# Stacking the meta rows of four heads on one operand's partitions, and regrouping the small steps of the input projection

## The reference

```python
h = rmsnorm(h_res, pre_mix_g)                     # (272, 2048)
q_da, k_da, v_da, q_g, k_g, v_g, g_g, lr_g = split_cols(h @ w_in)
o_da = diff_attention(...)    # 8 heads: p = softmax(q0 k0) - lam * softmax(q1 k1), causal; o = p @ v
                              # then rmsnorm over the head's 128 features
o_gla = gla(...)              # 4 heads, chunks of 64: A = tril(q_in k_in^T); o = A v + q_in S_prev
                              # then rmsnorm over the head's 256 features, times silu(g)
h_res = h_res + rmsnorm(concat[o_da, o_gla] @ w_out, post_mix_g)
y = conv_ffn(rmsnorm(h_res, pre_ffn_g), w_up, conv_w, conv_b, w_down)   # causal conv, width 3
h_res = h_res + rmsnorm(y, post_ffn_g)
return h_res[:, 16:]
```

## Time and profile before

| | |
|---|---|
| median of 3 runs | 1217.77 us (1217.37 to 1217.83) |
| the profiled execution | 1217.71 us, span 1216.0 us, mean granted clock 0.998 |
| input projection (96 slots) | to about 353 us of the span |
| PE, DVE, ACT, POOL busy | 1203.3, 662.5, 605.4, 478.2 us |

### The profile page before, as it was taken

One profiled execution on the slowest core, in us unless ns is written; L12 is line 12 of the kernel. 1 busy time (PEld: TensorE's weight loads), 2 busy tenths in 40 slices (PEclk: granted clock), 3 DMA queues, 4 the chain that ended last, 5 costly groups with the idle time before them and its releaser, 6 DMA issues.

```text
span 1216.0 us, 23728 instructions
## 1 busy us (share of the span) xinstructions
PE 1203.3 (99%) x8948; PEld 1145.3 (94%) x8948; DVE 662.5 (54%) x961; ACT 605.4 (50%) x908; POOL 478.2 (39%) x221
## 2 busy tenths in 40 slices
PE   9999999999999999999999999999999999999997
PEld 9999999999999999999999999999999988888885
DVE  7765555554565347766666666656656643232234
ACT  7544445455674447554445444444444544444444
POOL 1233333323424433444444444444444444444443
PEclk9999999999999999999999999999999999999999
DMA  9655554544536655566565565665655665665651
GB/s 330 201 156 156 141 161 143 148 130 132 153 124 197 193 164 159 173 189 182 178 185 177 177 188 174 188 186 168 193 181 169 191 203 184 199 191 189 197 166 70
DMA packets 175695, 212.31 MB, mean 175 GB/s; under 512 B 6688, under 2 KB 162720, under 8 KB 175520
## 3 DMA queue, kind: packets, MB, share of 16 engines
q1 hardware_dynamic: 175216, 210.32, 56.4%
q10 hardware_dynamic: 432, 1.34, 0.3%
HBM read 209.53 MB, written 2.10 MB: 174 GB/s over the span
## 4 chain that ended last, share of the span: by engine, by line
PE 95%; DVE 2%; ACT 2%; DMA 1%; issue 0%; SPq 0%; DVEq 0%; ACTq 0%
PE psum L416 69%; PE psum L1776 19%; PE psum L1416 1%; PE psum L1646 1%; DMA raw<-in_w_in 1%; PE psum L1476 1%; ACT w_hi L396 1%; PE psum L1804 0%; PE psum L1502 0%; PE psum L1736 0%; PE psum L1585 0%; DVE w_lo L400 0%; PE psum L1603 0%; PE psum L1503 0%; PE psum L1598 0%
## 5 line engine op out<-in xcount | busy, mean ns | idle before, releaser
L400 POOL TENSOR_TENSOR w_lo<-raw,w_hi 128x1024 fp32r<-128x1024 f32 x188 | 463.6, 2466 | 709.3 <-ACT w_hi L396 709.3
L416 PE MATMUL psum<-a_hi,w_hi 128*128 128x258 f32 (+1 forms) x2360 | 675.3, 286 | 0.9 <-ACT temp L594 0.8
L416 PE MATMUL psum<-a_lo,w_hi 128*128 128x258 f32 (+1 forms) x2360 | 673.8, 286 | 0.0
L416 PE MATMUL psum<-a_hi,w_lo 128*128 128x258 f32 (+1 forms) x2360 | 670.1, 284 | 0.0
L396 ACT ACTIVATE w_hi<-raw 128x1024 fp32r<-128x1024 f32 x391 | 411.5, 1059 | 471.6 <-PE psum L416 341.9
L400 DVE TENSOR_TENSOR w_lo<-raw,w_hi 128x1024 fp32r<-128x1024 f32 x204 | 268.7, 1318 | 412.9 <-ACT w_hi L396 411.7
L416 PEld LDWEIGHTS psum<-a_hi,w_hi 128*128 128x128 f32 x2360 | 448.3, 190 | 7.1 <-issue 4.3
L416 PEld LDWEIGHTS psum<-a_lo,w_hi 128*128 128x128 f32 x2360 | 448.5, 190 | 0.0
L416 PEld LDWEIGHTS psum<-a_hi,w_lo 128*128 128x128 f32 x2360 | 446.1, 189 | 0.1
L1306 DVE SCALAR_TENSOR_TENSOR proj<-proj,par 128x256 f32<-128x256 f32 x88 | 111.4, 1266 | 36.1 <-ACT proj L816 36.1
L1776 PE MATMUL psum<-w_hi,a_lo 128*128 128x512 f32 x336 | 130.7, 389 | 0.0
(11 more groups left out here) (234 smaller groups left out, 610.8 us busy)
## 6 DMA issues: line engine op xcount, KB each, us to landing
raw<-in_w_up SPq DMA_DIRECT2D x176, 512.0 KB, 3.6
raw<-in_w_in SPq DMA_DIRECT2D x95, 512.0 KB, 4.5
raw<-in_w_down SPq DMA_DIRECT2D x88, 512.0 KB, 4.1
raw<-in_w_out SPq DMA_DIRECT2D x32, 512.0 KB, 3.7
xT<-in_features SPq DMA_DIRECT2D x3, 544.0 KB, 7.6
temp<-in_post_ffn_g ACTq DMA_DIRECT2D x1, 1024.0 KB, 4.8
out<-proj SPq DMA_DIRECT2D x2, 512.0 KB, 2.7
out<-proj SPq DMA_DIRECT2D x4, 256.0 KB, 2.9
```

Of the source, the lines that this page charges most:

```text
L400: eng.tensor_tensor(w_lo[:, j % SPLIT, :], raw[:, j, :], w_hi[:, j % SPLIT, :], ALU.subtract)\
L416: mm = pe.matmul(psum[:, bank + m, 0:t1 - t0], w[:, j % SPLIT, cols], a[:, k, t0:t1], start=(k == 0 and step == 0), stop=(k == KT - 1 and ...
```

## The change

The 16 meta rows of four heads are put on partitions 0, 32, 64 and 96 (and the 15 after each) of one operand (`rows_of`). For the attention heads `v_meta_rows` then holds two groups of four heads, and `pT_meta_rows` gets one buffer for each of the four positions, zero elsewhere. `c_T` transposes the probabilities of four heads at once, and DVE multiplies them by a block mask (`row_block`) into `c_p_blocks`, so that `c_attend` is two matmuls of 128 rows by 8 columns; `c_attend_rest` is gone. For the GLA heads ACT copies the meta rows of v into `m_v` in every `v_T` step, DVE writes the masked products into `m_a`, and one step `m_o` in slot 89 (two matmuls of 128 rows by 8 columns) takes the place of line 1608 in four steps.

The steps move: `c_scores` 61 to 57, `c_T` 64 to 60, `c_attend` to 63, `c_sums` 67 to 65; DVE's and ACT's part of the normalization is split over slots 66 and 67; `da_o_T` from 69-76 to 68, 73, 73, 76, 81, 81, 84, 89; `gla_o` of the first three heads from +7 to +8, its normalization to +9 and `gla_o_T` from +10 to +11; `m_sums` 92 to 91. The weight stream, its order and its buffers are as they were.

```diff
-    for name, at in (("c_scores", C_BASE), ("c_T", C_BASE + 3), ("c_attend", C_BASE + 4), ("c_attend_rest", C_BASE + 5),
-                     ("c_sums", C_BASE + 6)):
+    for name, at in (("c_scores", C_SLOT), ("c_T", C_T_SLOT), ("c_attend", C_ATTEND_SLOT), ("c_sums", C_SUMS_SLOT)):
         if slot == at:
             steps.append((name, 0))
-    if C_BASE + 8 <= slot < C_BASE + 8 + n_da:
-        steps.append(("da_o_T", slot - C_BASE - 8))
+    steps += [("da_o_T", h) for h in range(n_da) if DA_O_SLOTS[h] == slot]
     for hd in range(n_gla):
-        for name, lag in (("v_T", 0), ("k_T", 3), ("kv", 5), ("gla_o", 7), ("gla_o_T", 10)):
+        for name, lag in (("v_T", 0), ("k_T", 3), ("kv", 5), ("gla_o", o_lag(hd)), ("gla_o_T", o_lag(hd) + 3)):
             if slot == gla_base(hd) + lag:
                 steps.append((name, hd))
+    if slot == M_O_SLOT:
+        steps.append(("m_o", 0))
     if slot == M_SLOT:
         steps.append(("m_sums", 0))
     return steps
...
-            "attend": 1, "c_scores": 2, "c_T": 1, "c_attend": 1, "c_attend_rest": 0, "c_sums": 1, "m_sums": 1, "da_o_T": 1, "v_T": 2, "k_T": 2, "kv": 2, "gla_o": 2,
+            "attend": 1, "c_scores": 2, "c_T": 1, "c_attend": 1, "c_sums": 1, "m_o": 1, "m_sums": 1, "da_o_T": 1, "v_T": 2, "k_T": 2, "kv": 2, "gla_o": 1,
             "gla_o_T": 2}
-C_BASE = 61
+C_SLOT, C_T_SLOT, C_ATTEND_SLOT, C_SUMS_SLOT = 57, 60, 63, 65
+DA_NORM_SLOT = 66
+DA_O_SLOTS = (68, 73, 73, 76, 81, 81, 84, 89)
 X_RMS_SLOT, LR_SLOT = 8, 9
 FIRST_LO = 12
 N_WARM = 12


 SCAN_SLOTS = (14, 16, 20, 22)
-M_SLOT = 92
+M_O_SLOT, M_SLOT = 89, 91


...
     return 60 + 8 * hd
+
+
+def o_lag(hd):
+
+    return 8 if hd < 3 else 7
...
-        m_o = sb("m_o", [P, n_gla, 2, NM])
-        m_sq = sb("m_sq", [P, n_gla, 2, NM])
+        m_o = sb("m_o", [P, 2, n_gla, NM])
+        m_sq = sb("m_sq", [P, 2, n_gla, NM])
+        m_a = sb("m_a", [P, n_gla, NM])
+        c_p_blocks = sb("c_p_blocks", [P, 2, 4, NM])
+        row_block = sb("row_block", [P, 4])
...
         pT_main = pv_buf[:, 2 * P:5 * P]
-        pT_meta_rows = pv_buf[:, 5 * P:7 * P]
-        pT_meta = pT_meta_rows[0:n_meta, :]
+        m_v = pv_buf[:, 5 * P:7 * P].rearrange("p (v e) -> p v e", v=2)
         o_nat = carve(2 * n_da * P).rearrange("p (t h e) -> p t h e", t=2, h=n_da)
-        v_meta_rows = tile(40, 4)[:, 0:n_da * P].rearrange("p (h e) -> p h e", h=n_da)
-        v_meta = v_meta_rows[0:n_meta]
+        stacked = tile(40, 5)[:, 0:10 * P]
+        v_meta_rows = stacked[:, 0:2 * P].rearrange("p (g e) -> p g e", g=2)
+        pT_meta_rows = stacked[:, 2 * P:10 * P].rearrange("p (j k) -> p j k", j=4)
+
+        def rows_of(n):
+
+            return slice(32 * (n % 4), 32 * (n % 4) + n_meta)
+
         c_e = tile(T_V + 7)[0:NM, 0:2 * n_da * n_meta].rearrange("p (c k) -> p c k", k=n_meta)
-        c_p = tile(T_K + 7)[0:NM, 0:n_da * n_meta].rearrange("p (h k) -> p h k", h=n_da)
-        c_pT = tile(T_K + 7)[0:n_meta, n_da * n_meta:(n_meta + NM) * n_da]
+        c_p_rows = tile(T_K + 7)[0:NM, 0:n_da * 32]
+        c_p = c_p_rows.rearrange("p (h k) -> p h k", h=n_da)[:, :, 0:n_meta]
...
+            link(masked(row_block[:], 1.0, [[-32, 4]], 0, 1, ALU.is_ge, 0.0))
+            pool.affine_select(out=row_block[:], in_=row_block[:], compare_op=ALU.is_ge, fill=0.0, base=n_meta - 1,
+                               pattern=[[32, 4]], channel_multiplier=-1).then_inc(consts_made, 1)
+            pool.memset(m_a[:], 0.0).then_inc(consts_made, 1)
...
-                    pool.memset(v_meta_rows, 0.0).then_inc(meta_zeroed, 1)
-                    pool.memset(pT_meta_rows, 0.0).then_inc(meta_zeroed, 1)
+                    pool.memset(stacked, 0.0).then_inc(meta_zeroed, 1)
+                    pool.memset(m_v, 0.0).then_inc(meta_zeroed, 1)
                 for hd in range(n_gla):
...
+                        copy(v_meta_rows[rows_of(h), h // 4, :], psum[0:n_meta, bank_of(step), 0:P]).then_inc(free(step), 1)
...
-                        copy(pT_meta, psum[0:n_meta, bank_of(step, 1), 0:2 * P]).then_inc(free(step, 1), 1)
-                if slot == C_BASE:
+                        copy(pT_meta_rows[rows_of(h), h % 4, :], psum[0:n_meta, bank_of(step, 1), 0:2 * P]).then_inc(free(step, 1), 1)
+                if slot == C_SLOT:
                     act_e.wait_ge(c_shifted, 1)
                     act_e.activation(c_e, c_e, ACT.Exp, scale=da_scale).then_inc(c_exps, 1)
-                if slot == C_BASE + 3:
-                    step = ("c_T", 0)
-                    await_full(act_e, step)
-                    copy(c_pT, psum[0:n_meta, bank_of(step), 0:NM * n_da]).then_inc(free(step), 1)
-                if slot == C_BASE + 6:
-                    act_e.wait_ge(da_ms_ready, 1)
-                    act_e.activation(o_ss[:], o_ss[:], ACT.Sqrt).then_inc(da_rms_ready, 1)
+                if slot == C_SUMS_SLOT:
                     step = ("c_sums", 0)
                     await_full(act_e, step)
                     act_e.wait_ge(eps_made, 1)
                     act_e.activation(c_rstd[:], psum[:, bank_of(step), 0:NM * n_da], ACT.Sqrt, scale=1.0 / da_e,
                                      bias=eps[:]).then_inc(free(step), 1)
-                if 0 <= slot - C_BASE - 8 < n_da:
-
-                    h = slot - C_BASE - 8
-                    step = ("da_o_T", h)
-                    await_full(act_e, step)
-                    act_e.activation(tile(T_Q + h)[:, NM:NQ], psum[:, bank_of(step), 0:seq], ACT.Copy,
-                                     scale=sub_gain[:]).then_inc(free(step), 1)
+                if slot == DA_NORM_SLOT:
+                    act_e.wait_ge(da_ms_ready, 1)
+                    act_e.activation(o_ss[:], o_ss[:], ACT.Sqrt).then_inc(da_rms_ready, 1)
+                for h in range(n_da):
+                    if slot == DA_O_SLOTS[h]:
+                        step = ("da_o_T", h)
+                        await_full(act_e, step)
+                        act_e.activation(tile(T_Q + h)[:, NM:NQ], psum[:, bank_of(step), 0:seq], ACT.Copy,
+                                         scale=sub_gain[:]).then_inc(free(step), 1)
                 for hd in range(n_gla):
...
+                            copy(m_v[rows_of(hd), v, :], src[META, 0, :])
                             copy(vg_nat[64:P, 0, v * P:(v + 1) * P], src[64:P, 0, :]).then_inc(free(step, v), 1)
...
                     link(dve.tensor_reduce(c_max[:], c_e, AX.X, ALU.max))
...
+                if slot == C_T_SLOT:
+                    step = ("c_T", 0)
+                    dve.wait_ge(consts_made, 9)
+                    await_full(dve, step)
+                    for g in range(2):
+                        ins = dve.tensor_tensor(c_p_blocks[:, g],
+                                                psum[:, bank_of(step), NM * g:NM * g + NM].unsqueeze(1).broadcast_to([P, 4, NM]),
+                                                row_block[:].unsqueeze(2).broadcast_to([P, 4, NM]), ALU.mult)
+                    ins.then_inc(free(step), 1)
+                if slot == C_ATTEND_SLOT:
                     step = ("c_attend", 0)
                     await_full(dve, step)
                     dve.tensor_copy(c_o[:], psum[:, bank_of(step), 0:NM * n_da]).then_inc(free(step), 1)
                     await_evacuated(dve, step)
                     dve.tensor_tensor(c_o_sq[:], c_o[:], c_o[:], ALU.mult).then_inc(c_squared, 1)
+                if slot == DA_NORM_SLOT:
                     dve.wait_ge(o_ss_ready, 1)
                     dve.tensor_scalar(o_ss[:], o_ss[:], 1.0 / da_e, EPS, ALU.mult, ALU.add).then_inc(da_ms_ready, 1)
-                if slot == C_BASE + 6:
+                    await_evacuated(dve, ("c_sums", 0))
+                    link(dve.reciprocal(c_rstd[:], c_rstd[:]))
+                    by_head = lambda t: t[:].rearrange("p (h q) -> p h q", q=NM)
+                    dve.scalar_tensor_tensor(out=halos(T_Q, 0), in0=by_head(c_o), scalar=sub_gain[:],
+                                             in1=by_head(c_rstd), op0=ALU.mult, op1=ALU.mult).then_inc(c_written, 1)
+                if slot == DA_NORM_SLOT + 1:
                     dve.wait_ge(da_rms_ready, 1)
                     link(dve.reciprocal(o_ss[:], o_ss[:]))
                     for t in range(2):
                         dve.tensor_tensor(o_nat[:, t], o_nat[:, t],
                                           o_ss[:, t * n_da:(t + 1) * n_da].unsqueeze(2).broadcast_to([P, n_da, P]),
                                           ALU.mult).then_inc(da_scaled, 1)
-                    await_evacuated(dve, ("c_sums", 0))
-                    link(dve.reciprocal(c_rstd[:], c_rstd[:]))
-                    by_head = lambda t: t[:].rearrange("p (h q) -> p h q", q=NM)
-                    dve.scalar_tensor_tensor(out=halos(T_Q, 0), in0=by_head(c_o), scalar=sub_gain[:],
-                                             in1=by_head(c_rstd), op0=ALU.mult, op1=ALU.mult).then_inc(c_written, 1)
                 for hd in range(n_gla):
```

(80 more changed lines are left out.)

5 lines of the change are left out of this document (2 added, 3 removed).

## The result

| | before | after |
|---|---|---|
| median | 1217.78 us (1217.37 to 1217.99, 8 runs) | 1221.06 us (1219.97 to 1222.31, 8 runs) |
| profiled execution, span | 1217.71 us, 1216.0 us | 1221.22 us, 1219.4 us |
| mean granted clock | 0.998 | 0.997 |

The ratio of the medians is 1.0028 (95% interval 1.0019 to 1.0038). The changed kernel is 3.3 us slower, 4.0 us above the forecast of 1217.1 and 1.2 us above the top of the range.

A forecast was written before the change was run, and what follows sets the result against it. It took TensorE, busy 99% of the span with 95% of the chain, to bound the kernel. 1217.71 - 4.0 gain + 0.6 + 2.4 + 0.4 of new waits = 1217.1 us; range 1213.8 to 1219.9.

The forecast's parts named there:

- line 1608, four heads: TensorE no longer issues the products of the two meta queries per GLA head: saves 0.53 each, 2.12 us.
- c_attend and its rest: Slots 65 and 66: the old matmuls, 2.15 us, go; two stacked matmuls at 0.45 take their place.
- m_o: New step of two stacked matmuls on TensorE, adding 0.4 us (0.26 to 0.6).
- c_T: Two transposes with 128 columns instead of eight with 16 on TensorE: saves 0.15 us.
- the wait of slot 71: k_T's 0.46 us wait behind DVE's evacuation of gla_o_T goes, as k_T reuses v_T's banks from slot 68.
- slot 68, wait for `da_scaled`: TensorE's da_o_T(0) waits for DVE's scaling of o_nat: 0.6 us if nothing comes between.
- slots 71, 79, 87: k_T waits for DVE's k_dec behind ACT's longer chain: together 2.4 or 0.7 us, 2.4 taken.
- chunk 98: Slots 91 to 98: two more ACT table loads outrun the slack at gla_o_T(3), adding 0.4 us (0 to 0.9).
- The gain: What TensorE saves by issuing and waiting less, net of the new steps: 4.0 us (3.6 to 4.4).
- the choice between 0.6 and 2.8: Slot 68's wait: 0.6 us if DVE's products run uninterrupted, 2.8 if POOL's split comes first or between; 0.6 taken.
- Rival B: POOL's split gets in at slot 68, making the wait 2.8 instead of 0.6: 1219.3 us, chance 0.25.
- The disputed point: Slots 71, 79, 87: whether POOL's split holds up DVE's og scaling; waits 2.4 us if so, 0.7 if not.

The follow-up runs named there:

- x2_one_product: The changed kernel with DVE's scaling of o_nat in slot 67 as one product of 2048 elements instead of two of 1024: 1217.90 us.
- x1_da69: The changed kernel with only the first da_o_T moved from slot 68 to 69: 1216.91 us.
- x3_busy68: The changed kernel with 11 filler matmuls on TensorE ahead of the wait for the scaling in slot 68: 1220.00 us.
- x5_da69_lag7: The changed kernel with the first da_o_T in slot 69 and gla_o of all heads back at +7, gla_o_T at +10: 1214.61 us.
- x8_products_first: The changed kernel with the first da_o_T in slot 69 and, in slots 69, 77, 85, DVE making q_in, k_in, k_dec before scaling og: 1215.32 us.
- x4_da69_m92: The changed kernel with the first da_o_T in slot 69 and m_sums back in slot 92: 1215.59 us.

## Why the prediction was wrong

The balance, term by term (us on the end of the span; "after" is read from the prices of the kernel after):

| term | forecast | after |
|---|---|---|
| line 1608, four heads | -2.12 | -2.12 |
| c_attend and its rest | -1.70 | -1.74 |
| m_o | +0.40 | +0.45 |
| c_T | -0.15 | -0.10 |
| the wait of slot 71 | -0.46 | -0.57 |
| c_sums and differences under 0.1 | 0 | -0.19 |
| slot 68, wait for `da_scaled` | +0.6 | +2.72 |
| slot 68, clock | not there | +1.63 |
| slots 71, 79, 87 | +2.4 | +2.2 |
| chunk 98 | +0.4 | +1.05 |
| sum | -0.6 | +3.3 |

**The gain was right**, 4.0 forecast and 4.27 found. The form of the stacked product could be priced from m_sums: c_attend's four records, timeline of the kernel after,

```profile
231.51 0.51 PE L1553 MATMUL psum<-c_p_blocks,proj 128*128 128x8 f32 x4
231.88 0.53 PE L1443 MATMUL psum<-ident,proj 128*128 128x128 f32 x3
```

start the next step 0.37 later, 0.09 each, between the two rows that the prediction had (0.07 and 0.12). The figure of the Trainium skill (TensorE: Matmul & The Clock Gate, LDWEIGHTS), about P/1.2 ns, gave 0.11 each and a gain smaller by 0.3; this trace does not bear that out for these records, though transposes of 128 columns do stand at 0.11. What had made c_attend dear before was the number of its records, 16 at 0.12, and the ends of a step of its own.

**The step that failed is slot 68**, twice over.

First, the choice between 0.6 and 2.8. The prediction named the mechanism, the two bounds and the point that decides (whether POOL's split starts before the second product is under way), and took the wrong end. Its counting was right: DVE first, by 0.24 where 0.1 to 0.2 was said; asked for at about +3.1, scaled at +3.6 if alone, and x2_one_product shows the 0.6. What it misjudged was the boundary. The earlier trace rows had one case of each kind, and the argument that these products have no wait between them, like those of the case where POOL was held, did not hold. Of the two cases of the earlier trace rows it was the one behind a long operation (3.13, behind DVE's split of 1.23 at 974.16) that repeated: measured here 3.20, and 3.21 in x1_da69. Why POOL got in here and not at the three boundaries of the other case (3.70) no run shows. Rival B, at 0.25, had this wait to a tenth (2.8 against 2.72).

Second, **the clock, which was in no term, bound or rival**. Rival B's 1219.3 takes the wait for its own length. The run shows that a wait of 2.6 us also slows what comes behind it: 1.6 in the slot, shown by x3_busy68 to go when TensorE is kept busy. Had the rival carried it, it would have stood at 1220.9 (1219.3 + 1.6), or 1220.5 with the 0.4 that slot 71 gives back; the median is 1221.06.

**Slots 71, 79, 87** were right in mechanism and nearly in size: 0.7, 0.7, 1.1 forecast, 0.41, 0.58, 1.22 found. The 0.41 owes something to luck: without the slow clock of slot 68 it is 0.83 (x2_one_product, x3_busy68). The disputed point, whether a tensor_scalar with its operands in SBUF is held up by POOL's split, went the way the sum took it. L1203 on DVE in the kernel after (durations ns), and one case of it with the split beside it:

```profile
L1203 DVE TENSOR_SCALAR temp<-temp,og_ss x8: 341/352/876, 263.7 to 352.1; 128x256 f32<-128x256 f32 x8
...
263.70 1.13 DVE L1203 TENSOR_SCALAR temp<-temp,og_ss 128x256 f32<-128x256 f32 x2
...
262.03 2.39 POOL L415 TENSOR_TENSOR w_lo<-raw,w_hi 128x1024 fp32r<-128x1024 f32 x1 [11.61 <-ACT w_hi L411]
```

The pair takes 1.13 instead of the 0.62 of the earlier trace rows, the first alone 0.88, ending at 264.58, just behind POOL's split (264.42). It matches the rule that the prediction took from the Trainium skill (SBUF — State Buffer, Who interferes with whom), which until then no row showed for tensor_scalar. x5_da69_lag7 and x8_products_first add what the ladder left unsaid: the wait for k_dec was a matter of the order on DVE, and the lag of 8 made it.

**Chunk 98**, forecast at 0.4 at gla_o_T(3), cost 1.05, and elsewhere. The mechanism, two more table loads of 1.28 between roots and silu, is right (x4_da69_m92). The slack was measured at the first user of the late root, and there it did suffice: slot 94 costs 0.43 and 0.44 before. It ran out further down the same queues, at the a_lo split of chunk 98. The prediction named this ("everything on ACT behind it starts later too") and bounded it at 0.9, a little short of the 1.05; its sum had 0.4.

In all: -4.27 + 4.35 + 2.2 + 1.05 = +3.3. Three moves in the slot table turned a gain of 4 us into a loss of 3.
